# The opening of a two-layer decoder trunk: order of the first loads, of x's transposes and of the angle arithmetic

## The reference

```python
for layer in range(DEPTH):
    h = rms_norm(x, ln1_g[layer])
    (a_q, a_ckv, a_kr, i_q, i_k, i_w, b_u, c_q, c_kv, c_gate) = jnp.split(h @ w_in[layer], offsets, axis=-1)
    a_out = dsa_mixer(...)      # top-k sparse attention with rotary parts (cos, sin of positions)
    b_out = s5_mixer(...)       # complex diagonal state space, exp/cos/sin of lambda * step
    c_out = nsa_mixer(...)      # compressed, selected and window attention
    mixed = jnp.concatenate([rms_norm(a_out, gain_a[layer]), rms_norm(b_out, gain_b[layer]),
                             rms_norm(c_out, gain_c[layer])], axis=-1)
    x = x + mixed @ w_out[layer]
    z = rms_norm(x, ln2_g[layer]) @ w_up[layer]
    x = x + jnp.square(jax.nn.relu(z)) @ w_down[layer]
return rms_norm(x, final_g)
```

## Time and profile before

| | |
|---|---|
| median of three runs | 647.29 us (647.24 to 649.35) |
| the profiled execution | 650.41 us, its span 648.7 us |
| granted TensorE clock, mean | 0.995 |
| TensorE busy | 616.9 us, 95% |
| VectorE busy | 429.3 us, 66% |
| ScalarE busy | 361.6 us, 56% |
| GpSimd busy | 231.8 us, 36% |
| moved by DMA | 102.79 MB, mean 158 GB/s |
| chain that ended last | TensorE 73%, VectorE 14%, ScalarE 5% |

### The profile page before, as it was taken

One profiled execution on the slowest core, in us unless ns is written; L12 is line 12 of the kernel. 1 busy time (PEld: TensorE's weight loads), 2 busy tenths in 40 slices (PEclk: granted clock), 3 DMA queues, 4 the chain that ended last, 5 costly groups with the idle time before them and its releaser, 6 DMA issues.

```text
span 648.7 us, 11260 instructions
## 1 busy us (share of the span) xinstructions
PE 616.9 (95%) x4268; PEld 531.6 (82%) x4268; DVE 429.3 (66%) x796; ACT 361.6 (56%) x672; POOL 231.8 (36%) x403
## 2 busy tenths in 40 slices
PE   5999988999999999999999999799999999999995
PEld 4867865689998889899888797568999899889984
DVE  7599898486655696765576786837765555554553
ACT  5765678836547534434456647984654443553451
POOL 5899358603245999910004303772000000000001
PEclk9999998999999999999999999999999999999998
DMA  9593804144954547376538640323475566546621
GB/s 260 160 256 104 160 2 115 33 158 145 319 196 138 192 153 246 120 237 190 190 96 264 145 131 2 82 67 99 146 256 192 182 198 189 185 173 200 195 97 66
DMA packets 55440, 102.79 MB, mean 158 GB/s; under 512 B 12713, under 2 KB 18906, under 8 KB 55354
## 3 DMA queue, kind: packets, MB, share of 16 engines
q1 hardware_dynamic: 48986, 96.04, 47.5%
q0 software_dynamic: 1792, 4.07, 2.6%
q10 hardware_dynamic: 4608, 1.97, 1.2%
HBM read 99.69 MB, written 1.31 MB: 156 GB/s over the span
## 4 chain that ended last, share of the span: by engine, by line
PE 73%; DVE 14%; ACT 5%; issue 3%; POOL 2%; DMA 1%; SPq 0%; DVEq 0%; POOLq 0%; ACTq 0%
PE pb L1756 71%; DVE w_lo L1318 5%; ACT tab_zone L1117 1%; ACT w_hi L872 1%; DVE dtmp L1239 1%; POOL dtmp L796 1%; DVE sc_zone L1643 1%; ACT ptmp L1130 1%; DMA raw<-in_w_in 1%; DVE dtmp L1519 1%; PE pb L1777 1%; DVE top L1515 1%; PE pb L1900 1%; DVE z_lo L1693 1%; DVE proj L1691 1%
## 5 line engine op out<-in xcount | busy, mean ns | idle before, releaser
L1318 DVE TENSOR_TENSOR w_lo<-raw,w_hi 128x1024 fp32r<-128x1024 f32 (+2 forms) x176 | 221.0, 1271 | 133.1 <-ACT w_hi L872 132.3
L872 ACT ACTIVATE w_hi<-raw 128x1024 fp32r<-128x1024 f32 (+2 forms) x184 | 187.5, 1027 | 191.4 <-PE pb L1756 165.3
L1756 PE MATMUL pb<-h_hi,w_hi 128*128 128x256 f32 x512 | 145.5, 284 | 1.3 <-DVE w_lo L1318 1.1
L1756 PE MATMUL pb<-h_hi,w_lo 128*128 128x256 f32 x512 | 144.9, 283 | 0.0
L1756 PE MATMUL pb<-h_lo,w_hi 128*128 128x256 f32 x512 | 144.9, 283 | 0.0
L1756 PEld LDWEIGHTS pb<-h_hi,w_hi 128*128 128x128 f32 x512 | 98.2, 192 | 3.4 <-issue 2.3
L1756 PE MATMUL pb<-w_hi,z_hi 128*128 128x512 f32 x256 | 100.1, 391 | 0.7 <-DVE w_lo L1318 0.7
L1756 PE MATMUL pb<-w_hi,z_lo 128*128 128x512 f32 x256 | 99.8, 390 | 0.0
L1756 PE MATMUL pb<-w_lo,z_hi 128*128 128x512 f32 x256 | 99.6, 389 | 0.0
L1756 PEld LDWEIGHTS pb<-h_hi,w_lo 128*128 128x128 f32 x512 | 98.2, 192 | 0.4
L1756 PEld LDWEIGHTS pb<-h_lo,w_hi 128*128 128x128 f32 x512 | 98.2, 192 | 0.0
(11 more groups left out here) (309 smaller groups left out, 850.8 us busy)
## 6 DMA issues: line engine op xcount, KB each, us to landing
raw<-in_w_up SPq DMA_DIRECT2D x64, 512.0 KB, 3.8
raw<-in_w_down SPq DMA_DIRECT2D x64, 512.0 KB, 4.3
raw<-in_w_in SPq DMA_DIRECT2D x24, 512.0 KB, 4.8
raw<-in_w_out SPq DMA_DIRECT2D x8, 512.0 KB, 3.9
raw<-in_w_out SPq DMA_DIRECT2D x16, 256.0 KB, 4.0
raw<-in_w_in SPq DMA_DIRECT2D x8, 308.0 KB, 3.0
raw<-in_w_in SPq DMA_DIRECT2D x8, 280.0 KB, 2.9
x<-in_x ACTq DMA_DIRECT2D x4, 256.0 KB, 4.2
```

The lines of the kernel that those rows point to most:

```text
L872: hi_made.by(act.activation(w_hi[:, n % RING, 0:width(n)], raw[:, n % RING, 0:width(n)], ACT.Copy))
L1318: lo_made.by(dve.tensor_tensor(w_lo[:, n % RING, 0:width(n)], raw[:, n % RING, 0:width(n)], w_hi[:, n % RING, 0:width(n)].bitcast(F32), AL ...
L1756: return pe.matmul(o, l, r, start=start, stop=stop, skip_group_check=True)
```

## The change

Nothing is computed differently. In the opening of layer 0:
- SyncE issues only log_step, ln1 and lambda_re in front of piece 0. Positions, `gain_c` and `gain_a` go between pieces 0 and 1, three rows of `vrow_b` between 1 and 2, the rest between 2 and 3. lambda_im and ln2 are issued by ScalarE behind x's block 0. `craw`, `braw` and the matrices follow pieces 4, 5 and 7.
- ScalarE issues x's block 0 first, blocks 1 and 2 behind the table load, block 3 behind the first two `h_hi`. The high part of piece 0 stands in front of `h_hi` 0 and 1; pieces 2 and 3 in front of `h_hi` 4 and 5; s5's sines in front of 6 and 7; the squares and the sines of the angles move in among pieces 4 to 7.
- VectorE makes the low part of a piece ahead of its `h_lo`; the angles move from the beginning to between pieces 5 and 6, and `turn` behind piece 7.
- TensorE turns block 0 at the start and the other three between the two halves of pieces 0, 1 and 2. Each half waits for its own `h_lo`.
- GpSimd's `rstd` of x stands behind all powers.
- `tk` is cleared by a ScalarE copy of zeros behind piece 13 instead of a VectorE memset, and SyncE waits for it before the DMAs into `tk`.

```diff
@@ sync
-            sp.dma_start(pos_i[:], ...)
-            sp.dma_start(step_rows, ...)
-            sp.dma_start(vrow_a[0:8], ln1_g...)
-            sp.dma_start(vrow_a[8:16], s5_lambda_re...)
-            sp.dma_start(vrow_a[16:24], s5_lambda_im...)
-            sp.dma_start(vrow_a[24:32], ln2_g...)
...
-            first_pieces(0, lambda q: None)
...
+            def rows(q):
+                if q == 0:
+                    (step_rows, vrow_a[0:8] ln1_g, vrow_a[8:16] s5_lambda_re)
+                if q == 1:
+                    (pos_i, gain_c x2, row(0, gain_a))
+                if q == 2:
+                    for r, src in ((2, gain_b), (8, kv_norm_g), (9, s5_glu_b)):
+                        row(r, src)
+                if q == 3:
+                    (vrow_b[11:13] s5_d, cmp_pos_k, cmp_pos_v)
+            first_pieces(0, rows)
...
+                        if L == 0 and n == 5:
+                            load_c(sp, 0)
+                        if L == 0 and n == 6:
+                            load_b(sp, 0, first0)
+                        if L == 0 and n == 8:
+                            load_params(sp, 0, params0, ("rows",))
...
                         if L == 0 and n == 24:
+                            sp.wait_ge(tk_clear.sem, 1)
                             lags_in(sp, L)
@@ gpsimd, prep_powers
                     step(double(pw, n, n))
-                    if occ == 0 and n == 2:
-                        rstd(0, 1, r1[:], stat[:, 0:2], D_MODEL)
                 tt(pa[:, 0], pw[:, 0], pmag[:], ALU.mult, False)
                 prep_a.by(pool.tensor_tensor(pa[:, 1], pw[:, 1], pmag[:], ALU.mult))
+                if occ == 0:
+                    rstd(0, 1, r1[:], stat[:, 0:2], D_MODEL)
@@ scalar
-            for b in range(4):
-                (load x block b)
-            load_b(act, 0, first0)
+            load_x(0)
+            act.dma_start(vrow_a[16:24], s5_lambda_im...).then_inc(rows_a.sem, 16)
+            act.dma_start(vrow_a[24:32], ln2_g...).then_inc(rows_a.sem, 16)
             act.wait_ge(zeros.sem, 1)
             step(act.activation(sp[:, 23, :], half_neg[:], ACT.Exp))
+            load_x(1)
+            load_x(2)
...
-                for n in range(4):
-                    if L == 0:
-                        h_parts(L, 0, g1[:, L], (2 * n, 2 * n + 1))
-                    hi(L, n)
-                    if L == 0 and n == 0:
-                        act.wait_ge(lrs_s5.sem, lrs_s5.at(0, 1))
-                        mag_s5.by(act.activation(sp[:, 1, :], sp[:, 21, :], ACT.Exp))
...
+                    hi(0, 0)
+                    h_parts(0, 0, g1[:, 0], (0, 1))
+                    load_x(3)
+                    hi(0, 1)
+                    act.wait_ge(lrs_s5.sem, lrs_s5.at(0, 1))
+                    mag_s5.by(act.activation(sp[:, 1, :], sp[:, 21, :], ACT.Exp))
+                    h_parts(0, 0, g1[:, 0], (2, 3))
+                    hi(0, 2)
+                    hi(0, 3)
+                    h_parts(0, 0, g1[:, 0], (4, 5))
+                    s5_trig(0)
+                    h_parts(0, 0, g1[:, 0], (6, 7))
...
-                    s5_trig(0)
+                    hi(0, 4)
+                    hi(0, 5)
+                    sums(0, 0, sq_sum.by)
+                    c_table(0, 1)
+                    hi(0, 6)
                     act.wait_ge(ang_rope.sem, 1)
                     step(act.activation(ang2[:], ang[:], ACT.Sin))
                     act.activation(ang[:], ang3[:], ACT.Sin).then_inc(trig_rope.sem, 1)
-                    sums(0, 0, sq_sum.by)
-                    c_table(0, 1)
-                for n in range(4, 6):
-                    hi(L, n)
+                    hi(0, 7)
+                    step(act.activation(sp[:, 23, :], half_neg[:], ACT.Tanh))
...
                 for n in range(12, 14):
                     hi(L, n)
+                if L == 0:
+                    tk_clear.by(act.activation(tk[:].rearrange("p g s n -> p (g s n)"), nmx[:, 0, 0:1].to_broadcast([PART, 8 * SEQ]), ACT.Copy))
@@ vector
-            (the thirteen operations of the angles)
-            for t in (tk,):
-                step(dve.memset(t[:], 0.0), False)
...
+                if L == 0:
+                    for n in range(2):
+                        lo(n)
+                        h_rest(0, g1[:, 0], lambda k: xT_rows(k, 0), first=2 * n, count=2)
+                    lo(2)
+                    lo(3)
+                    h_rest(0, g1[:, 0], lambda k: xT_rows(k, 0), first=4, count=2)
+                    den(0)
+                    h_rest(0, g1[:, 0], lambda k: xT_rows(k, 0), first=6, count=2)
...
+                for n in range(4, 6):
+                    lo(n)
                 if L == 0:
-                    den(0)
-                for n in range(4, 6):
+                    angles()
+                for n in range(6, 8):
                     lo(n)
                 if L == 0:
                     turn()
...
-                for n in range(6, 8):
-                    lo(n)
@@ tensor
+                def x_block(b):
+                    pe.wait_ge(x_loaded[b].sem, 16)
+                    for k in (2 * b, 2 * b + 1):
+                        for t in range(TT):
+                            m = x_turned(k, t, 0)
+                    xT_ps.by(m)
                 if L == 0:
-                    for b in range(4):
...
+                    x_block(0)
+                    first_vectors()
...
                         ready(n)
-                        if i == 0:
-                            pe.wait_ge(h_lo_made.sem, h_lo_made.at(L, 2 * q + 2))
                         for kk in range(2):
                             k = 2 * q + kk
+                            if i == 0:
+                                pe.wait_ge(h_lo_made.sem, h_lo_made.at(L, k + 1))
+                            if (L, i, kk) == (0, 0, 1) and q < 3:
+                                x_block(q + 1)
```

More of the change, by code:

```diff
@@ L522, in _ @@
-            sp.dma_start(vrow_b[11:13], s5_d.rearrange("l (k g) h -> k l (g h)", k=2)).then_inc(rows_b.sem, 16)
-            for r, src in ((13, cmp_pos_k), (29, cmp_pos_v)):
-                sp.dma_start(vrow_b[r:r + 16], src.rearrange("l (q r) d -> q l (r d)", r=2)).then_inc(rows_b.sem, 16)
-            load_c(sp, 0)
-            load_params(sp, 0, params0, ("rows",))
+            def rows(q):
+                if q == 0:
+                    sp.dma_start(step_rows, s5_log_step.rearrange("l (j g) -> j l g", g=2)).then_inc(step_row.sem, 16)
+                    sp.dma_start(vrow_a[0:8], ln1_g.rearrange("l (k p) -> k l p", p=PART)).then_inc(rows_a.sem, 16)
+                    sp.dma_start(vrow_a[8:16], s5_lambda_re.rearrange("l (j g) p -> j l (g p)", g=2)).then_inc(rows_a.sem, 16)
+                if q == 1:
+                    sp.dma_start(pos_i[:], positions.rearrange("o (t p) -> p (o t)", p=PART)).then_inc(pos_loaded.sem, 16)
+                    for g in range(C_KV):
+                        sp.dma_start(vrow_b[4:8, :, HD * g:HD * g + HD],
+                                     gain_c.rearrange("l (g j d) -> g j l d", g=C_KV, d=HD)[g]).then_inc(rows_b.sem, 16)
+                    row(0, gain_a)
+                if q == 2:
+                    for r, src in ((2, gain_b), (8, kv_norm_g), (9, s5_glu_b)):
+                        row(r, src)
+                if q == 3:
+                    sp.dma_start(vrow_b[11:13], s5_d.rearrange("l (k g) h -> k l (g h)", k=2)).then_inc(rows_b.sem, 16)
+                    for r, src in ((13, cmp_pos_k), (29, cmp_pos_v)):
+                        sp.dma_start(vrow_b[r:r + 16], src.rearrange("l (q r) d -> q l (r d)", r=2)).then_inc(rows_b.sem, 16)
@@ L527, in _, with row @@
+            def row(r, src):
+                sp.dma_start(vrow_b[r:r + src.shape[1] // PART], src.rearrange("l (k p) -> k l p", p=PART)).then_inc(rows_b.sem, 16)
+            first_pieces(0, rows)
             for L in range(DEPTH):
@@ L879, in sums, with load_x @@
                 s(m)
-            for b in range(4):
+            def load_x(b):
                 cols = slice(b * SEQ, (b + 1) * SEQ)
```

76 lines of the change are left out of this document (31 added, 45 removed).

## The result

The changed kernel takes 649.69 us (median of 9 executions, 648.77 to 650.09), the kernel before 648.13 us in the same comparison (9 executions, 646.74 to 649.35): ratio 1.0025, 95% interval 1.0016 to 1.0034. That is 1.6 us slower, where +0.3 to +0.4 was forecast. The direction and the main mechanism held, the size didn't, and the forecast of 647.6 missed the median by 2.1 us in two parts: 0.84 because the median on which it stood (647.29, of three executions) was low, 1.25 because the sum was too small. The prediction took 0.5% as about what a measurement can tell; the interval here is 0.1% to either side.

A forecast was written before the change was run, and what follows sets the result against it. The opening was taken as bound by TensorE's start, then VectorE's long queue from 24.94 us. VectorE's start -3.0, angles +2.95, idle +0.35 and tk 0 to 0.1 gave +0.3 to +0.4 us on 647.29: 647.6, range 645.5 to 649.8.

The forecast's parts named there:

- Part 1: Start of weight piece 0: fewer small DMAs in front of it, so TensorE starts at about 9.4 instead of 11.93, gaining 2.5 us.
- Rival E: Rows behind x on ScalarE's queue land as late as now, so TensorE starts at 10.9: 649.1 us, chance 0.05.
- Part 2: x's transposes inside TensorE's first tile shrink the 2.5 us gain to 1.1 us; piece 3 ends at 25.0 against 26.1.
- Rival C: TensorE's slow pace ends at 17 as now, not 14.3, since it rests longer first; 1.2 us lost: 648.8, chance 0.12.
- the rule weighed: TensorE's throttled clock is the default, activity releases it at a varying moment; so fast pace could come no earlier than now.
- Part 3: Chain through ScalarE and VectorE: piece 4 3.0 us earlier, angles eat it, piece 8 +0.3 us; bounds -0.7 to +1.8.
- VectorE's start -3.0: VectorE takes up the low part of piece 4 at 21.9 instead of 24.94, 3.0 us earlier.
- +2.95 + 0.35: Angles between pieces 5 and 6 add 2.95 us to VectorE's queue, and its idling before piece 7 adds 0.35.
- Part 4: Clearing tk on ScalarE, about 2.0 us, moves relu by about 1.5 but costs 0 to 0.1 us at the end.
- Part 5: GpSimd's powers wait for sines at 19.5; 1.2 us delay against 0.87 slack gives +0.3, in VectorE's shadow.
- Rival D: GpSimd becomes the bound, slowed by VectorE's low parts: typically +1.5, up to +3.3 (650.6); chance 0.15 for over 1 us.
- Rival B: The gain survives: VectorE takes up piece 4 at 20.9 without the gap before piece 7, -1.1: 646.0, chance 0.23.

The follow-up runs named there:

- a_again: The changed kernel executed again with no edit: 649.60 us against 648.36 for the kernel before, ratio 1.0022.
- b_third: The kernel before, unedited, profiled a third time: 647.94 us in its one execution.
- b_again: The kernel before executed once more with no edit: 648.31 us against 648.32, ratio 1.000.
- a_angles_gap: The changed kernel with the angles in VectorE's idle time before piece 1's low part instead of behind piece 5: 648.98 us, ratio to the kernel before 1.0013.
- v3: The changed kernel with six moves, among them angles before piece 1's low part and squares behind h blocks 4 and 5: 647.02 us, ratio to before 0.9982.
- a_warm: The changed kernel with fifteen more identity transposes on TensorE before tile 0, their result unread: 649.06 us, ratio to the kernel before 1.0016.
- v4: v3 with fifteen more identity transposes on TensorE before tile 0: 649.46 us, ratio to the kernel before 1.0012.
- a_x_front: The changed kernel with x's four blocks issued first and all sixteen transposes before tile 0: 651.23 us, ratio to the kernel before 1.0040.
- a_tk_vector: The changed kernel with tk cleared by a VectorE memset at its start again: 650.36 us, ratio to the kernel before 1.0032.
- b_angles_late: The kernel before with only the angles, their sines and turn moved to where the change has them: 651.19 us against 648.36, ratio 1.0051.
- v5: v3 with GpSimd's rstd of x right behind the powers, as in the changed kernel: 649.17 us against 648.54 for the kernel before, ratio 1.0004.
- b_rows: The kernel before with only the change's order of small row loads on SyncE and ScalarE: 652.34 us against 648.54, ratio 1.0060.

## Why the prediction was right, and where its size was not

**Part 1** held. Piece 0 is issued at 1.92 (1.95) and its high part starts at 6.34 (6.65), the vectors are copied at 5.34 (6.25), TensorE starts at 9.20 (9.4). Rival E is out.

**Part 2** held in its result, 25.16 for tile 1 (25.0), but by luck, for two errors cancel. The slow pace ended at 12.2, not at 14.3. But the later pieces came late, which the prediction didn't cost at all: 1.92, 3.93, 5.32 and 7.04 are their issues, and piece 1 took 7.2 us and piece 3 8.4, with ScalarE idle for 3.06 and 0.96. Rival C, the pace that stays slow until 17, doesn't appear in after's two profiles (12.2 and 15.1), though a_again's rise stands at the prediction's own mark of 15. Its time of 648.8 (+1.5) is near the +1.6 measured, but by chance, for its cause isn't there. What the rule weighed there gets right is that the moment varies; that it could come no earlier than in the one execution at hand doesn't follow, since before itself has 10.0, 15.1 and 17.0.

**Part 3** is where the size failed. Its steps held to the tenth: piece 4 at 22.08 (21.9), idle before piece 7 0.45 (0.35), piece 8 at 32.58 (32.6), TensorE idle 1.74 before it (2). The failed term is "VectorE's start -3.0", 24.94 taken as the usual moment of before. It is 23.92 in b_third and 22.02 in b_again, so the term is -1.8 or 0, since the forecast 21.9 of after hardly moves (22.08, 22.55). The other side of the term, +2.95 + 0.35 = 3.3 from piece 4 to piece 8, measures 10.50 - 6.96 = 3.5 against b_third. Sum against b_third: -1.8 + 3.5 = +1.7 at piece 8 and +1.6 at piece 17. With the rise at 15.1 on both sides (a_again) it is -1.4 + 3.7 = +2.3 at piece 8 and +2.2 at piece 17, so that the first sum equals the 1.6 of the medians is partly luck in the pair. Both are far above the +0.3 forecast; the part's own bounds, -0.7 to +1.8, hold the 1.6. That this execution stood 3.1 us above the median was said in the prediction, and it was read as an offset of the whole. But of the 2.5 us of span by which it stands above b_third, 1.0 is there at piece 17, out of the very rows of the sum; the other 1.4 were lost between 219 and 293 us.

**The attribution** inside part 3 was incomplete. The angles were called the cause, and a_angles_gap shows ScalarE's squares and the copy of C (3.1 us) standing beside them, so that taking the angles away returned 0.7 us and not 3. That the squares alone would return as little is argued, not shown.

**Part 4** held for after: no difference, though it was the copy's place in ScalarE's wait for TensorE that hid it, and the relu wasn't moved by it. **Part 5** held: powers from 19.07 (19.5 for the sines), rotations to 68.03 (68.7). In the timeline of after VectorE waits there for TensorE and not for GpSimd:

```profile
66.63 0.74 DVE L1348 TENSOR_TENSOR w_lo<-raw,w_hi 128x560 fp32r<-128x560 f32 x1 [0.94 <-ACT w_hi L886]
68.32 0.39 DVE L1485 COPY ytok<-pb 128x224 f32<-128x224 f32 x1 [0.95 <-PE pb L1792]
```

Rival D is out, for its place at the rotations. GpSimd is a bound in before where the clock rises early: in b_again VectorE waits 1.27 us at 39.28 for its `bd`, which is why that execution, 1.8 us ahead of b_third at piece 8, is only 1.0 ahead at piece 17.

**Rival B**, the gain that survives, is out for after. v3 ends near its price (-1.3 us, -1.1 at B), but it is another kernel and gets there otherwise: VectorE takes up piece 4 at 21.90, not at 20.9, and the angles are out of the closed queue. (B's -1.1 on the median is 646.2, not the 646.0 written.)

## What to carry to other kernels

Before a term is taken as the difference of two moments in one profile, ask what decides each moment: where it hangs on the moment at which TensorE's clock rises, take it from several executions, for the term can be -3.0 in one and 0 in another. When work is moved into a closed queue, price every engine on which something was moved into the same stretch, since two additions side by side hide each other, and removing one can return little (0.7 of 3 us here). And a row can't be moved behind a large load without moving all that waits for it: the order of loads and the order of the engine that reads them are one edit.

## What the runs showed of the hardware

- The moment at which the clock reaches 2.4 GHz differs between executions of one program by 7 us here (10.0 to 17.0 for before), and with it piece 17 by 2.0 us (60.66 and 62.70). It can rise behind transposes alone, as at 7.3 in a_warm and at 10.0 in b_again, but the same work doesn't always raise it: v4, busy with transposes from 3.84 to 8.69, has the rise at 13.6, and a_x_front, with x's twelve from 10.63 to 13.45, at 19.6.
- TensorE can fall back to half speed in the middle of dense stretches, behind a rest, but the rest alone doesn't decide it. A rest of 2.1 to 2.3 us near 100 us, which all fourteen executions have, was followed by such a stretch in nine and by none in five (b_third, b_again, after, a_angles_gap, v3). It cost little there: before stands 1.02 us behind b_third at piece 17 and 1.03 at piece 20, with the stretch between them. Earlier in the kernel only the longer rests were followed by one. The busy time by stretches of a_again (columns as in the earlier trace rows) shows it after a rest of 1.94 us before 34.60; the same came after 1.94 in a_tk_vector, 3.38 in b_angles_late and 2.56 in v5, and didn't after 1.74 in after and 1.76 in a_warm:

```profile
34.00:36.00 2.00, 1.40 (x5) 1.19 (x6) 1.90 (x7) 1.06 (x1) 1.84 (x4) 0.88 0.40 56
36.00:38.00 2.00, 2.00 (x6) 1.52 (x6) 1.90 (x7) 0.90 (x1) 1.80 (x5) 0.50 0.94 297
38.00:40.00 2.00, 2.00 (x11) 1.57 (x10) 1.99 (x2) 0.49 (x3) 1.69 (x2) 0.76 0.28 28
```

- The column PEclk shows 1.00 in the first windows even where the steps come at 0.43 us; in the opening the pace has to be read from the matmuls themselves.
- A row of 8 KB takes 6.7 us when it is issued behind 1 MB on the same queue, and positions of 1 KB, issued at the same moment behind piece 0 of 512 KB, take 4.1 us in after, where one of x's blocks has been issued by then, and 5.6 in b_rows and 8.1 in a_x_front, where x's four are issued one behind the other; issued first of all, as in before, they take 3.0.
